# Second returned expert row of each token added by VectorE instead of by TensorE's diagonal products

## What is computed

```python
def layer_norm(x, g, b):
    mu = mean(x); var = mean((x - mu) ** 2)
    return (x - mu) * rsqrt(var + LN_EPS) * g + b

for l in range(2):
    m = hybrid_mixer(h, ...)
    h = layer_norm(ALPHA * h + m, ln1_g[l], ln1_b[l])
    f = grouped_moe(h, ...)        # 32 experts, two of them per token
    h = layer_norm(ALPHA * h + f, ln2_g[l], ln2_b[l])

# grouped_moe, for one token with experts e0, e1 and weights w0, w1 (w0 + w1 = 1):
#   f = w0 * expert_e0(h) + w1 * expert_e1(h)
```

## Time and profile before

| | us |
|---|---|
| median of 3 runs | 2209.92 |
| lowest and highest run | 2207.26, 2210.29 |
| time of the profiled execution | 2212.06 |
| its span, first to last instruction | 2210.3 |
| TensorE (PE) busy in it | 2006.5 |
| VectorE (DVE) busy | 959.5 |
| ScalarE (ACT) busy | 672.1 |
| GpSimd (POOL) busy | 212.8 |

### The profile page before, as it was taken

How to read it: one execution, slowest core, us unless ns; L and a number is a source line. 1 busy time by engine, 2 the same in 40 slices (tenths; PEclk the granted TensorE clock), 3 DMA queues, 4 the chain that set the end, 5 groups by cost and what they waited for, 6 DMA issues and landing times.

```text
span 2210.3 us, 30445 instructions
## 1 busy us (share of the span) xinstructions
PE 2006.5 (91%) x10004; PEld 1223.4 (55%) x10012; DVE 959.5 (43%) x1898; ACT 672.1 (30%) x1358; POOL 212.8 (10%) x244
## 2 busy tenths in 40 slices
PE   6999999999979988788899999999998899887787
PEld 5777777877743332223376777778777333222232
DVE  5756865846651111011256668657566311110113
ACT  3545554645210000000143536646551010000000
POOL 3000002000011111111000000110001111111100
PEclk9999999999989999999999999999999999999999
DMA  5321321323689999999942113113148899999996
GB/s 174 115 77 39 115 77 39 115 77 121 263 325 422 426 424 427 426 426 421 385 153 77 39 61 118 53 40 138 52 154 333 344 426 425 426 424 426 426 419 269
DMA packets 104200, 535.63 MB, mean 242 GB/s; under 512 B 14800, under 2 KB 17744, under 8 KB 83552
## 3 DMA queue, kind: packets, MB, share of 16 engines
q1 hardware_dynamic: 92064, 510.41, 57.6%
q0 software_dynamic: 11968, 23.11, 2.8%
HBM read 527.17 MB, written 23.07 MB: 249 GB/s over the span
## 4 chain that ended last, share of the span: by engine, by line
PE 72%; DMA 10%; DVE 8%; issue 4%; ACT 2%; another core or an unknown queue 2%; SPq 1%; DVEq 0%; ACTq 0%; POOLq 0%
PE ps L1189 17%; PE ps L832 12%; PE ps L834 11%; PE ps L833 11%; PE ps L1209 7%; DMA wslot<-in_w_up 7%; PE ps L951 3%; PE ps L981 2%; PE ps L1012 2%; PE ps L1179 1%; DMA spare<-in_w_up 1%; DMA h<-h_rows 1%; DVE scr L2293 1%; ACT scr L1429 1%
## 5 line engine op out<-in xcount | busy, mean ns | idle before, releaser
L2273 DVE COPY scr<-ps 128x512 f32<-128x512 f32 x64 | 44.3, 692 | 727.4 <-PE ps L1179 727.4
L832 PE MATMUL ps<-hT_lo,w_hi 128*128 128x512 f32 (+1 forms) x816 | 329.7, 404 | 12.0 <-DVE w_lo L1724 11.8
L834 PE MATMUL ps<-hT_hi,w_hi 128*128 128x512 f32 (+1 forms) x816 | 320.1, 392 | 0.0
L833 PE MATMUL ps<-hT_hi,w_lo 128*128 128x512 f32 (+1 forms) x816 | 319.4, 391 | 0.0
L1372 ACT ACTIVATE scr<-ps 128x512 f32<-128x512 f32 (+1 forms) x214 | 111.2, 524 | 536.5 <-PE ps L1209 308.8
L1190 PE MATMUL ps<-scr 128*64 128x512 f32 x480 | 221.4, 616 | 0.0
L1209 PE MATMUL ps<-ring,scr 128*64 128x512 f32 x736 | 168.1, 598 | 33.3 <-DVE scr L2293 33.3
L1660 ACT ACTIVATE scr<-ps 64x512 f32<-64x512 f32 x64 | 37.7, 589 | 507.9 <-PE ps L1190 507.9
L1724 DVE TENSOR_TENSOR w_lo<-ring,w_hi 128x1024 fp32r<-128x1024 f32 x114 | 139.5, 1223 | 100.1 <-ACT w_hi L1392 95.0
L832 PEld LDWEIGHTS ps<-hT_lo,w_hi 128*128 128x128 f32 (+1 forms) x816 | 154.0, 189 | 47.9 <-issue 15.8
L1392 ACT ACTIVATE w_hi<-ring 128x1024 fp32r<-128x1024 f32 x114 | 120.3, 1055 | 188.0 <-PE ps L834 133.9
(11 more groups left out here) (269 smaller groups left out, 3329.5 us busy)
## 6 DMA issues: line engine op xcount, KB each, us to landing
ring<-in_w_down SPq DMA_DIRECT2D x42, 2048.0 KB, 46.8
ring<-in_w_in SPq DMA_DIRECT2D x30, 2048.0 KB, 8.2
scr<-in_w_up SPq DMA_DIRECT2D x26, 2048.0 KB, 50.9
xslot<-in_w_up SPq DMA_DIRECT2D x14, 2048.0 KB, 43.2
spare<-in_w_gate SPq DMA_DIRECT2D x14, 2048.0 KB, 47.5
ring<-in_w_gate SPq DMA_DIRECT2D x12, 2048.0 KB, 43.0
scr<-in_w_gate SPq DMA_DIRECT2D x12, 2048.0 KB, 44.6
h<-in_w_gate SPq DMA_DIRECT2D x12, 2048.0 KB, 46.2
```

Source lines behind the costliest of these rows:

```text
L832: mm(out, a[0], b[1], start=first, stop=False)
L833: mm(out, a[1], b[0], start=False, stop=False)
L834: return mm(out, a[0], b[0], start=False, stop=last)
```

## The change

TensorE keeps the residual and the first returned row of each token. VectorE multiplies the second row by its weight, adds the bank to it and writes the result into `h`, half a tile at a time. It then takes the statistics from `h` and centres in one instruction over 1024 columns, as the other norms do. Four diagonals are made instead of eight. VectorE now waits itself for the second row's load.

```diff
-        weigh = scr[:, 14336:14336 + 2 * NT * P].rearrange("p (n c) -> p n c", c=P)
+        weigh = scr[:, 14336:14336 + NT * P].rearrange("p (n c) -> p n c", c=P)
...
                     for half in range(2):
                         b = c_bank(t, half)
-                        for k in range(2):
-                            pe.wait_ge(got_land[t][k].sem, got_land[t][k].at("y", l))
-                            ins = mm(bank[b].t, weigh[:, 2 * t + k, :], got[t][k][:, half * 512:(half + 1) * 512],
-                                     start=False, stop=(k == 1))
+                        pe.wait_ge(got_land[t][0].sem, got_land[t][0].at("y", l))
+                        ins = mm(bank[b].t, weigh[:, t, :], got[t][0][:, half * 512:(half + 1) * 512],
+                                 start=False, stop=True)
                         filled(ins, b, ("c", t, half))
...
-                    if key == "ln2":
-
-                        for half in range(2):
-                            b, cut = c_bank(t, half), slice(half * 512, (half + 1) * 512)
-                            V.scalar_tensor_tensor(h[:, t, cut], bank[b].t, moments[:, t, 0:1], ln_params[key][0][:, cut],
-                                                   ALU.subtract, ALU.mult).then_inc(bank[b].read, 1)
-                        for half in range(2):
-                            in_sbuf(c_bank(t, half), ("c", t, half), l)
-                    else:
-                        link(V.scalar_tensor_tensor(h[:, t, :], h[:, t, :], moments[:, t, 0:1], ln_params[key][0],
-                                                    ALU.subtract, ALU.mult), l)
+                    link(V.scalar_tensor_tensor(h[:, t, :], h[:, t, :], moments[:, t, 0:1], ln_params[key][0],
+                                                ALU.subtract, ALU.mult), l)
...
                         if t < NT:
+                            dve.wait_ge(got_land[t][1].sem, got_land[t][1].at("y", l))
                             for half in range(2):
-                                b = c_bank(t, half)
+                                b, cut = c_bank(t, half), slice(half * 512, (half + 1) * 512)
                                 filled(b, ("c", t, half), l)
-                                half_stats(t, half, bank[b].t)
+                                V.scalar_tensor_tensor(h[:, t, cut], got[t][1][:, cut], wts_keep[:, 1, t:t + 1],
+                                                       bank[b].t, ALU.mult, ALU.add).then_inc(bank[b].read, 1)
+                                in_sbuf(b, ("c", t, half), l)
+                                half_stats(t, half)
...
                     for t in range(NT):
-                        for k in range(2):
-                            ins = V.tensor_scalar(weigh[:, 2 * t + k, :], ident, wts_keep[:, k, t:t + 1], None, ALU.mult)
+                        ins = V.tensor_scalar(weigh[:, t, :], ident, wts_keep[:, 0, t:t + 1], None, ALU.mult)
```

## The result

| us | before | changed kernel |
|---|---|---|
| median of the runs | 2209.92 (5 runs, 2206.81 to 2212.74) | 2219.48 (5 runs, 2216.99 to 2221.53) |
| ratio, 95% interval | | 1.0049 [1.0035, 1.0063] |
| profiled execution, its span | 2212.06, 2210.3 | 2221.53, 2219.7 |
| first layer's stage | 48.50 | 53.27 |
| last layer's stage | 29.17 | 32.19 |

The account below looks back on a forecast made before the run. VectorE bounds the norm's length, TensorE's products only its start. Last layer 4 x 1.74 - 1.99 = +5.0, first layer 4 x 1.74 - 0.83 - 1.16 = +5.0, sum +9.9: 2219.8 us, range 2215 to 2223.5.

Parts of the forecast that it names:

- TensorE's 6.9 us a layer: Returned-row products: 16 fewer instructions of 0.434 us per layer; most of it saved on an engine ahead of VectorE anyway.
- The first bank, -0.87: Last layer, first tile: two product instructions fewer ahead of the first bank, so VectorE gets it 0.87 us earlier.
- The second bank, -1.12: Last layer, first tile: VectorE's 1.02 us wait for the second bank goes, worth 1.12 us with its lost overlap.
- The diagonals, -0.83 in the first layer, nothing in the last: VectorE makes four diagonals, not eight: the first layer's norm starts 0.83 us earlier; the last layer gains nothing.
- The adds, 1.54: Two new weigh-and-adds per tile on VectorE: 2.98 us to the aggregate instead of 1.44, so +1.54 per tile.
- The late rstd, +0.20: Per tile: centring with two SBUF inputs makes GpSimd's rstd take 1.42 us, not 0.55, costing VectorE +0.20 us.
- The slack of 1.16 us in the first layer: First layer, third tile: VectorE may end its transposes' low part 1.16 us later before TensorE's value products wait.
- Over 9 us per tile: First layer: VectorE's period with the transposes' low parts, leaving room for value products some 2 us longer at lowered clock.
- rstd was late: Its rival, rstd not late in the returned rows' norm: +5.9 us, 2215.8 us; chance 0.10.
- the second fall: Rival: TensorE's clock falls once more ahead of the first layer's third tile, adding 2.2 us: +12.1, 2222.0 us; chance 0.06.
- The adds weren't covered: Its rival, added VectorE work lies in waits for TensorE: the kernel gains 3.98 us, 2205.9 us; chance 0.04.
- The first layer's shift wasn't taken up later: Its rival, slack in a later wait absorbs the first layer's shift, leaving the last layer's +5.0: 2214.9 us; chance 0.10.

Follow-up runs that it names:

- the kernel with one row: The kernel before, with the second returned row left out of products and diagonals and no adds; median 2205.74 us, ratio 0.999.
- the second profile: The changed kernel run again as it is, nothing altered; median 2219.07 us, ratio 1.0047 to the kernel before.
- the kernel with both adds first: The changed kernel with both weigh-and-adds of a tile ahead of both its statistics; median 2218.11 us, ratio 1.0038 to the kernel before.
- the kernel with doubled products: The changed kernel with the first returned row's product run twice; median 2264.42 us, but routing differs, so only stages count: 53.32 and 35.34 us.

## Why the prediction was right

Predicted +9.9 us; the medians say +9.6 and +8.7, the stages +4.8 and +4.7. Point by point:

- **TensorE's 6.9 us a layer are not the gain.** Right. Both ways: without half the products the stages fell by 3.8 us, not 13.9; with them put back under the adds the first layer didn't move.
- **The first bank, -0.87.** Right: 10.56 to 9.70 us behind the residual's first product in the kernel with one row and in the second profile of the changed one, and with the residual's 1.70 us evened also in its first.
- **The second bank, -1.12.** Right in the changed kernel, where no wait is left in the first tile. I gave as its reason that the bank is there before VectorE needs it; without the adds that isn't so (0.16 us of wait, and 0.86 in place of 1.12).
- **The diagonals, -0.83 in the first layer, nothing in the last.** Right, 12.57 to 11.74 us (11.82 in the second profile).
- **The adds, 1.54.** Measured 1.56, shown by the rows of three kernels. The choice of 0.03 us instead of 0.20 behind each add was right: statistics 0.77 to 0.78 behind the add. The bound with the pair's 0.66 us is what the kernel with both adds first gives.
- **The late rstd, +0.20.** The mechanism is shown by three kernels, the size was too large: 0.12 us per tile, since VectorE waits 0.44 to 0.46 us and not 0.53 as in the mixer's norm. Why it waits less isn't shown. Of the terms in the sum this is the one that was mis-sized clearly; eight times 0.08 is 0.6 us.
- **The slack of 1.16 us in the first layer.** Right: 6.78 - 0.83 - 4.77 = 1.18. The 1.2 us of the kernel with one row belong to another place, the first tile.
- **A working that was wrong and cost nothing.** "Over 9 us per tile" divides a stretch of four tiles' norms and three low parts by three. VectorE's tiles in it began 4.66, 6.27 and 6.58 us apart, and with the change 6.36, 7.94 and 8.31. That was still room enough for the slower value products.
- **The rivals.** rstd was late, eight times. TensorE's clock did fall, once, where the pause was forecast (in the first profile until about 1120, 5.5 us, and in the second for less than 3 us), and it cost nothing, as counted; the second fall, ahead of the third tile, didn't come: the granted clock is 0.98 from 1120, and the third tile's transposes, from 1123.58 on, take 1.03 us where the second's took 1.96. The adds weren't covered. The first layer's shift wasn't taken up later: the time between the two stages changed by +0.44 us in the first pair of traces. One pair doesn't say much, since a kernel's untouched stretches differ by nearly 4 us (ahead of the first stage 1089.88 us in one profile of the changed kernel and 1086.12 in the other). But over the seven profiles with the same routing this time lies between 1036.8 and 1040.1 us, and it isn't shorter by 5 us where the first stage is longer by 5. The medians too would have stood near +5.

The prediction also named as a sign the time from the first layer's first returned product to the third tile's value products: 28.79 us before, 33.52 now, so +4.7 where 5 was forecast.

That the median came within 0.3 us of the prediction is partly luck: the scatter of medians is larger than that.

## What to carry to other kernels

Price a shift of work by who waits in the stage, not by the engines' shares of the span: VectorE was busy 43% of the time, TensorE 91%, and taking 13 us off TensorE for 9.5 us on VectorE lost 9.6 us, because the added work stands where VectorE sets the pace of the tile loop, or is only 1.2 us from doing so. Where a small GpSimd instruction stands in VectorE's chain, look at what VectorE does beside it. Placing an independent instruction with at most one SBUF input there hid its whole wait, in three tiles of four. And where the result of an instruction is waited for at once, putting an independent one of the same form in between is worth 0.12 us each time.

## What the runs showed beyond that

- The residual's 16 product instructions follow on a pause of some 2.1 to 2.4 us in both layers of seven profiles and in the first layer of the other two. Yet they take 7.10 us at full clock in three of these cases (both layers of the first profile of the changed kernel, the first layer of the kernel with doubled products) and 8.64 to 8.80 in the others, among them the same kernel's second profile. The granted clock after such a pause is thus not settled by the kernel, and one profile of each kernel would have put 1.7 us of it down to the change. What decides it stays open.
- The statistics take the same time from a bank and from h: 690 ns on average before, 692 after.
- The first-layer norm of the mixer has the same long rstd and a wait of 0.53 us in each of its tiles. Whether the same reordering would gain anything there is open, and I didn't try it: behind each of these tiles but the last VectorE waits for TensorE before the next add (0.31 us ahead of 600.61), so part of what rstd gives back may go into that wait.
- What an rstd made by VectorE itself would give was not measured. It would have to undercut a wait of 0.44 us a tile.
